# A two-layer hybrid attention block: attention products with the values as the stationary operand, probabilities scaled before them, and branch parts summed in PSUM

## The reference, cut to what matters

```python
y_a = _dsa_attention(...) @ w_branch_a[l]    # 4 heads, one key and value; 64 keys chosen by an index score
y_b = _moba_attention(...) @ w_branch_b[l]   # 4 heads, each with its own keys and values
# branch C: 8 heads in 2 groups; three softmaxes each, weighted by gates
o = g[..., 0:1] * o_c + g[..., 1:2] * o_s + g[..., 2:3] * o_w
```

## Time and profile before

| what | value |
|---|---|
| median of 3 runs | 1232.95 us (1232.95 to 1233.24) |
| the profiled execution | 1232.73 us, of which the span is 1230.8 us |
| PE busy | 1205.6 us (98%) |
| DVE busy | 720.9 us (59%) |
| ACT busy | 577.0 us (47%) |
| DMA, mean over the span | 172 GB/s |
| granted clock of TensorE | 0.999 of full speed |

### The profile page before, as it was taken

The page is one execution under the profiler, slowest core; times in us unless marked ns, Lnnn a source line. Parts: engine busy times, 40 slices in busy tenths (PEclk is TensorE's granted clock), DMA queues, the critical chain, the costliest instruction groups (busy, mean ns, idle before and its releaser), DMA issues.

```text
span 1230.8 us, 18004 instructions
## 1 busy us (share of the span) xinstructions
PE 1205.6 (98%) x6079; PEld 1004.4 (82%) x6079; DVE 720.9 (59%) x800; ACT 577.0 (47%) x733; POOL 47.5 (4%) x83
## 2 busy tenths in 40 slices
PE   5999999999999999999999999999999999999997
PEld 4888888888888888888878888888888888888886
DVE  3545456757775764545455545476676675645454
ACT  5444445446554354343454443454556535443433
POOL 2000000001000100000000000000000020000000
PEclk9999999999999999999999999999999999999999
DMA  6655554764333546555546555646543235655552
GB/s 221 236 176 198 174 200 138 226 214 138 103 104 136 171 157 213 177 190 185 173 139 233 176 194 181 204 152 191 193 145 104 104 137 171 205 182 193 180 195 86
DMA packets 148011, 212.17 MB, mean 172 GB/s; under 512 B 7936, under 2 KB 109424, under 8 KB 147952
## 3 DMA queue, kind: packets, MB, share of 16 engines
q1 hardware_dynamic: 146192, 209.97, 51.3%
q10 hardware_dynamic: 1760, 1.43, 0.4%
HBM read 210.33 MB, written 1.05 MB: 172 GB/s over the span
## 4 chain that ended last, share of the span: by engine, by line
PE 96%; DVE 1%; issue 1%; DMA 1%; ACT 0%; ACTq 0%; POOL 0%; DVEq 0%; SPq 0%; POOLq 0%
PE ps L1049 28%; PE ps L1051 28%; PE ps L1050 28%; PE ps L1276 3%; PE ps L1121 2%; PE ps L1229 1%; PE ps L1253 1%; PE ps L1065 1%; DMA raw<-in_ffn_w_up_dram 1%; PE ps L1292 1%; PE ps L1170 1%; DVE gates L641 0%; PE ps L1222 0%; PE ps L1174 0%; PE ps L1187 0%
## 5 line engine op out<-in xcount | busy, mean ns | idle before, releaser
L391 DVE TENSOR_TENSOR wlo<-raw,whi 128x2048 fp32r<-128x2048 f32 (+2 forms) x199 | 445.6, 2245 | 225.1 <-ACT whi L858 213.1
L1049 PE MATMUL ps<-whi,ht_hi 128*128 128x512 f32 (+1 forms) x1248 | 492.1, 394 | 4.5 <-DVE ht_lo L400 4.5
L1051 PE MATMUL ps<-whi,ht_lo 128*128 128x512 f32 (+1 forms) x1248 | 484.2, 388 | 0.0
L1050 PE MATMUL ps<-wlo,ht_hi 128*128 128x512 f32 (+1 forms) x1248 | 483.3, 387 | 0.0
L858 ACT ACTIVATE whi<-raw 128x2048 fp32r<-128x2048 f32 (+2 forms) x199 | 372.8, 1879 | 175.0 <-PE ps L1051 168.3
L1049 PEld LDWEIGHTS ps<-whi,ht_hi 128*128 128x128 f32 x1248 | 235.1, 188 | 50.4 <-DVE ht_lo L400 5.1
L1051 PEld LDWEIGHTS ps<-whi,ht_lo 128*128 128x128 f32 x1248 | 234.9, 188 | 49.1
L1050 PEld LDWEIGHTS ps<-wlo,ht_hi 128*128 128x128 f32 x1248 | 235.4, 189 | 45.3
L1049 PE MATMUL ps<-whi,at_hi 128*128 128x512 f32 x320 | 124.9, 390 | 0.0
L1051 PE MATMUL ps<-whi,at_lo 128*128 128x512 f32 x320 | 124.7, 390 | 0.0
L1050 PE MATMUL ps<-wlo,at_hi 128*128 128x512 f32 x320 | 124.5, 389 | 0.0
(11 more groups left out here) (150 smaller groups left out, 642.5 us busy)
## 6 DMA issues: line engine op xcount, KB each, us to landing
raw<-in_ffn_w_gate_dram SPq DMA_DIRECT2D x89, 512.0 KB, 3.7
raw<-in_ffn_w_up_dram SPq DMA_DIRECT2D x89, 512.0 KB, 4.7
raw<-in_ffn_w_down_dram SPq DMA_DIRECT2D x88, 512.0 KB, 3.8
raw<-in_w_in_dram SPq DMA_DIRECT2D x88, 512.0 KB, 4.4
raw<-in_w_out_dram SPq DMA_DIRECT2D x16, 512.0 KB, 3.9
raw<-in_w_branch_c_dram SPq DMA_DIRECT2D x8, 512.0 KB, 4.0
w_k<-in_cmp_w_k_dram SPq DMA_DIRECT2D x4, 512.0 KB, 6.6
raw<-in_w_branch_b_dram SPq DMA_DIRECT2D x4, 512.0 KB, 5.2
```

Of the source, the lines that this page charges most:

```text
L391: nc.vector.tensor_tensor(wlo[:, n, 0:w], raw[:, n, 0:w], whi[:, n, 0:w].bitcast(F32), ALU.subtract).then_inc(lo_done, 1)
L1049: nc.tensor.matmul(o, xh, wh, start=start, stop=False)
L1050: nc.tensor.matmul(o, xh, wl, start=False, stop=False)
L1051: return nc.tensor.matmul(o, xl, wh, start=False, stop=stop)
```

## The change

1. `weighted` is turned round. For each half of the keys and each of two heads, 64 columns of values are loaded as weights, and the turned probabilities stream past, 512 columns (first half of the keys) or 256 (second half). Head 0 of a couple writes partitions 0 to 63, head 1 partitions 64 to 127. Part B, whose heads have separate values, takes twice as many products of half the width. The result has the head's columns on partitions, as the branch matrices want it.
2. The division by the sum, and C's gates, move ahead of the product: `scaled` on DVE replaces `normed` and multiplies the probabilities, head by head, in eight instructions for each part (four of 128 elements, four of 256).
3. C, S and W of a group of heads are summed in PSUM. The order becomes I, C, B, S0, W0, S1, W1, A. C's product goes to the S parts, two of 256 columns in each.
4. `turn_out` for the attention outputs (16 transposes) is gone. `heads_out` (ACT) and `heads_rest` (DVE) split each finished bank, two of them in positions 4 and 6, two after position 9.
5. Order: the exponentials of the first half start after the first of the two maxima, the copies of pieces 0, 1 and 2 and the turning of pieces 1 and 2 move in each position, maxima come ahead of the copy on DVE.
6. The second quarter of the compressor's key matrix now lies in the space of the rotated inputs. SP loads it after all of them are turned, ahead of slab 18.

```diff
-PAIRS = ["I", "C", "B", "S0", "S1", "W0", "W1", "A"]
+PAIRS = ["I", "C", "B", "S0", "W0", "S1", "W1", "A"]
+ENDS = ["B", "W0", "W1", "A"]
...
-            def normed(l, e):
+            def scaled(l, e, t):
                 pair, b = PAIRS[e], e % 2
-                dve.wait_ge(o_ps, l * 7 + e)
                 own(l)
                 if pair == "C":
+                    dve.wait_ge(exp_done, l * 2 + 2)
...
+                    step(nc.vector.tensor_tensor(src, src, rden[:, b, :].unsqueeze(2).broadcast_to([P, 16, CPAD]),
+                                                 ALU.mult), ("scaled", e, 0))
                     return
+                dve.wait_ge(exp_half, l * 12 + 2 * (e - 2) + t + 1)
+                rd = rden[:, b, 4 * t:4 * t + 4]
+                step(nc.vector.reciprocal(rd, den[:, b, 4 * t:4 * t + 4]))
+                if pair not in "AB":
+                    g, br = int(pair[1]), 1 if pair[0] == "S" else 2
+                    own(l)
+                    step(nc.vector.tensor_tensor(rd, rd, cgt3[:, t, 4 * g:4 * g + 4, br], ALU.mult))
                 own(l)
+                for h in range(4):
+                    pv = prob_view(b, t)[:, h, :]
+                    step(nc.vector.tensor_scalar(pv, pv, rden[:, b, 4 * t + h:4 * t + h + 1], None, ALU.mult),
+                         ("scaled", e, t))
+            def heads_rest(l, n):
+                dve.wait_ge(heads_hi, l * 4 + n + 1)
+                hi, lo = (v[:, :, :].rearrange("p j c -> p (j c)") for v in heads_parts(n))
+                step(nc.vector.tensor_tensor(lo, ps[:, heads_bank(n), :], hi.bitcast(F32), ALU.subtract), ("heads", n))
...
                 for e in range(NPOS):
-                    if 1 <= e - 2:
-                        normed(l, e - 2)
...
+                    if e == 1:
+                        index_scores(l)
+                    if 0 < e < len(PAIRS):
+                        scaled(l, e, 0)
                     if e > 0:
                         convert(l, S + 17 + e)
+                    if 1 < e < len(PAIRS):
+                        scaled(l, e, 1)
                     for _ in range(rounds[e]):
...
             def weighted(l, e):
+                if pair[0] == "S":
+                    for j in range(2):
+                        hc = 4 * int(pair[1]) + 2 * j
+                        nc.tensor.matmul(o[:, j], v_blk[:, hc:hc + 2, :].rearrange("p h c -> p (h c)"), pc_t,
+                                         start=j == 0, stop=False, skip_group_check=True)
+                opens, vcol = pair in "AB", heads_of(pair)[3]
+                for kt in range(NT):
+                    pt = p_t[:, 2:3, :] if kt else p_t[:, 0:2, :]
+                    pt = pt.rearrange("p f (j e c) -> p e j f c", j=2, e=2)
+                    for js in ([slice(0, 1), slice(1, 2)] if pair == "B" else [slice(0, 2)]):
+                        for h in range(2):
+                            v0 = vcol(2 * js.start + h)
+                            ins = nc.tensor.matmul(o[h * HD:(h + 1) * HD, js, kt:NT, :], pr[:, kt, v0:v0 + HD],
+                                                   pt[:, h, js], start=opens and kt == 0 and js.start == 0,
+                                                   stop=kt == 1 and pair in ENDS, skip_group_check=True)
...
+                    if q == 5:
+                        sp.wait_ge(fill_ps, (l + 1) * NFILL)
+                        sp.dma_start(w1[0][1], rows_cols(cmp_w1_k, l, 8 * P, 8, 0, P)).then_inc(w1_in[0], 16)
                     load_halves(l, S + 13 + q, w_in, 512 * (q % 2), 4, M_G + 512 * (q // 2), 512)
```

More of the change, by code:

```diff
@@ L699, in mixer @@
                 assert done == 16
-                for n in range(4):
-                    turned_rest(l, n)
+                heads_rest(l, 2)
+                heads_rest(l, 3)
                 convert(l, S + 27)
@@ L708, in mixer @@
                 branch_out(l, 0, 2, range(0, 3))
-                turned_rest(l, 4)
-                turned_rest(l, 5)
+                turned_rest(l, 0)
+                turned_rest(l, 1)
                 branch_out(l, 0, 2, range(3, 4))
                 convert(l, S + 30)
-                for n in range(6, 8):
+                for n in range(2, 4):
                     turned_rest(l, n)
@@ L1001, in mixer @@
                         prob_out(l, e - 1, 0)
+                    if e == 4:
+                        heads_out(l, 0)
+                    if e == 6:
+                        heads_out(l, 1)
                     if e > 0:
                         convert(l, S + 17 + e)
[L1004 to L1005 removed]
                     if 0 < e < len(PAIRS):
                         exps(l, e)
[L1008 to L1009 removed]
+                    if e == len(PAIRS):
+                        prob_out(l, e - 1, 2)
                 gates(l, 5)
[L1011 to L1012 removed]
+                heads_out(l, 2)
+                heads_out(l, 3)
                 for m in range(27, 30):
                     convert(l, S + m)
[L1015 removed]
+                for n in range(2):
                     turned(l, n)
                 convert(l, S + 30)
[L1018 removed]
+                for n in range(2, 4):
                     turned(l, n)
@@ L1259, in weighted @@
                 pair = PAIRS[e]
+                n = next(n for n, p in enumerate(ENDS) if PAIRS.index(p) >= e)
                 pe.wait_ge(pt_a, l * PT_ACT + acts_before(e + 1))
-                if e > 1:
-                    wait_step(pe, l, ("pt", e))
-                    wait_step(pe, l, ("norm", e - 1))
-                if pair == "C":
-                    for t in range(NT):
-                        ins = nc.tensor.matmul(ps[:, 7 - t, :], p_t[:, 0, t * P:(t + 1) * P],
-                                               v_blk[:, :, :].rearrange("p h c -> p (h c)"), start=True, stop=True)
-                    ins.then_inc(o_ps, 1)
-                    return
@@ new lines, in weighted, with turn_z @@
+                ins.then_inc(o_ps, 1)
+            def turn_z(l, *pieces):
+                for n in pieces:
+                    wait_step(pe, l, ("z", 1 if n < 2 else 3))
+                    for j in range(2):
+                        for t in range(NT):
+                            k = 2 * n + j
+                            ins = nc.tensor.transpose(ps[:, 4 + n, j * SEQ + t * P:j * SEQ + (t + 1) * P],
+                                                      gate[:, t, 0, k * P:(k + 1) * P], ident[:, :])
+                    ins.then_inc(ot_ps, 1)
```

181 lines of the change are left out of this document (72 added, 109 removed).

## The result

The changed kernel takes 1239.06 us (median of 6 runs, 1238.4 to 1240.23) against 1232.95 (6 runs beside it, 1231.99 to 1236.02). The ratio is 1.0048, with a 95% interval of 1.0035 to 1.0061: it is slower, by 6.1 us, which is clear of the 0.2% that the prediction counted as no change. The forecast was 1232.1 with a range of 1227 to 1237.5, and "slower" had 0.20. The profiled execution took 1239.42 us, its span is 1237.7 us, and the granted clock of TensorE is 0.990 of full speed, where it was 0.999. All six runs show 0.990 or 0.991.

A forecast was written before the change was run, and what follows sets the result against it. PE, busy 98%, was taken as the bound. Its 7.9 us saving a layer goes nearly all into two waits for DVE, leaving 0.8 us in all: 1232.73 to 1231.9, plus 0.2 for the median, 1232.1 us; range 1227 to 1237.5.

The forecast's parts named there:

- PE's saving: Attention products 1.6 us a part instead of 2.63, and 16 output transposes gone: PE does 7.9 us less a layer.
- VectorE's prices and sum: DVE's multiplications at 0.21 and 0.27 us; its work from B's scaling to the mask sums to 53.6 us.
- The wait: At position 7 PE stands idle for DVE's mask, 6.8 us in each layer.
- C's turning: Early in the layer, PE waits 0.7 us for DVE's scaling of C before turning its probabilities.
- the quarter matrix: Its load was expected hidden ahead of `compress`; rival that it is late: 1.0 us a layer, 1234.1 us, chance 0.15.
- The step that failed: From the end of the mask wait to the first branch slab: 24.6 us instead of 27.99.
- the gain of 0.4 us a layer: The branch slab starts at 384.6 instead of 384.99, nearly all of PE's saving going into two waits; 0.8 us in all.
- a rule on VectorE's prices: Skill's errata figure for DVE multiplications, 0.13 and 0.19 us, each part 0.6 us cheaper; set aside for a trace row.
- The rivals: Cheap scaling (0.22), one element per cycle (0.09), heads not overlapping (0.06), late quarter matrix (0.15).
- VectorE at one element per cycle: DVE's scaling ahead of the mask runs at single rate, losing 3.6 us a layer: 1240.1 us, chance 0.09.
- L627's row: Trace row of a one-tensor DVE instruction, 384 elements in 0.359 us, taken as twice the rate: 0.067 us for 128.
- A mean of 59%: DVE's busy share of the whole span in the profile before; in position 6 it was busy 9.80 of 11.5 us.

The follow-up runs named there:

- Experiment 1: Changed kernel with 9 selection rounds in place of 16 (those of positions 5 and 6 left out), so the mask comes early: 1218.03 us.
- experiment 10: Changed kernel with GpSimd's gate multiplications of positions 3 and 5 held until the mask is made: 1235.9 us.
- experiment 2: Changed kernel with 30 unused products filling PE's wait ahead of A's mask: 1233.46 us.
- experiment 4: Changed kernel with 4 unused products ahead of each layer's first transposes and 8 behind them: 1236.29 us.
- Experiment 6: Changed kernel with 22 unused products in the mask wait and position 6's slab remainder moved behind the selection rounds on DVE: 1231.43 us.
- experiment 3: Changed kernel with position 7's slab ahead of A's scores, and the slabs of positions 8 and 9 ahead of the products they followed: 1224.76 us.
- experiment 5: Changed kernel with the slabs of positions 7 to 9 moved earlier on PE and position 6's slab remainder behind DVE's selection rounds: 1218.42 us.
- experiment 7: Changed kernel with only the first of four heads scaled in the five parts ahead of the mask: 1226.12 us.
- experiments 8: Changed kernel with slabs moved earlier, position 6's remainder late, and eight unused products behind each layer's first transposes: 1216.65 us.
- experiment 9: Control: the kernel before the change, with eight unused products behind each layer's first transposes: 1230.43 us.

## Why the prediction was wrong, by its own steps

**PE's saving: right.** A part's products take 1.45 us (forecast 1.6, before 2.63), and the transposes are gone. Experiment 1 shows it in the time: 1218.03 us when the mask is early.

**VectorE's prices and sum: right in mechanism, a little short, and helped by luck.** 0.20 and 0.27 us against 0.21 and 0.27. From B's scaling to the mask it was 54.4 us instead of 53.6. The positions came to 7.6, 10.0, 11.7, 11.8 and 13.3 us against 7.8, 9.65, 11.5, 11.2 and 13.5. The term that was missing is GpSimd's gate work, 0.5 us in position 3 and in position 5 (experiment 10). The mask was ready at 360.08, forecast 359.9. That the two agree to 0.2 us is luck in part: the changed kernel's profile starts 0.6 us earlier (19.50 against 20.08 us), and measured from the start of its own mixer the mask is 0.7 us later than forecast in layer one and 0.8 in layer two.

**The wait: right.** 7.2 us in each layer, forecast 6.8. C's turning waited 0.5 (forecast 0.7), and `compress` for nothing, so the quarter matrix was in time.

**The step that failed** is the one behind the wait: "Behind that wait, to the first branch slab, it was 384.99 - 357.00 = 27.99 us. It is now + 0.44 - 2 x 1.03 - 1.76, 24.6 us." I priced the wait by its length and took the work behind it at the speed that rows before show, though no row of the mixer before has such work behind seven idle microseconds. With the wait filled it is just 24.6 us (experiment 2). With PE idle the windows from 357 to 363 us show the lower level, and it is 26.2 in layer one and 26.8 in layer two. That is 1.6 and 2.1 us. With the mask's 0.7 and 0.8 it turned the gain of 0.4 us a layer into a loss of 1.9 in the first and 2.5 in the second.

The trace before did hold one place of the kind, unread: the program's start, where PE waits 6.7 and 3.1 us with eight transposes between, and the first slab's products then start 0.43 us apart instead of 0.23. It is a start-up, with hardly any work of PE before it, and a window over 15 to 20 us gives a clock of 1.00 there. So the pitch of the products was the only sign.

```profile
9.83 1.97 PE L1065 MATMUL ps<-ident,x 128*128 128x128 f32 x8 [6.71 <-POOLq L784]
...
14.89 0.79 PE L1049 MATMUL ps<-whi,ht_hi 128*128 128x512 f32 x1 [3.09 <-DVE ht_lo L400]
15.48 0.63 PE L1050 MATMUL ps<-wlo,ht_hi 128*128 128x512 f32 x1
```

The Trainium skill (TensorE: Matmul & The Clock Gate, HAM oscillation) says that a PE that waits falls back to half rate and begins its next stretch of work slow. The windows above agree for this wait of 7 us: 0.50 from 357 to 363 us. I had weighed a rule on VectorE's prices, and passed over this one, by which the forecast wait itself had a second price.

**The gap between the layers** was in no step. The stretch through it cost 3.1 us, again at the lower level (622 to 630 us). Where the clock holds there the loss is gone (experiment 2), or most of it, less the filler's own delay (experiment 4). The two mixers (1.6 and 2.1 us) and the gap (3.0) explain what lies between the changed kernel and experiment 2: 6.7, less 0.5 by which the changed kernel's profile started earlier, against 6.2 between the two profiles' spans and 5.6 between the medians. What is left of the miss, 1233.46 against 1232.1, is within the 1.5 us by which the two masks came late, and GpSimd's share of 1.0 us a layer covers that.

**The rivals.** None of them was the cause. The slower side had one mechanism of the right place and sign, VectorE at one element per cycle. It did not happen: the multiplication's two lengths differ by 0.07 us for 128 elements, as L627's row had said. The measured 1239.06 lies near that rival's 1240.1 by coincidence.

**What stays open** is why the clock falls in the gap in some executions of a kernel and not in others. All six runs of the changed kernel have 0.990 or 0.991. Experiment 6 lost it nine times in ten, and experiment 3 probably three times in four (told from the clocks of whole executions). How long PE waits there doesn't decide it: in the profiles the two waits of the gap add up to 2.6 to 2.7 us where the clock held (the kernel before, experiments 1, 2 and 3) and to 2.7 to 2.9 where it fell (the changed kernel, experiments 5, 6, 7 and 10), with 2.73 us (experiment 3) among the first and 2.67 (experiment 10) among the second. The same goes for the waits of 2.7 us in experiment 7. The cost differs too: against the kernel before, the stretch through the gap took 1.6 us (experiment 7) to 3.1 us more (the changed kernel). Experiment 2 never lost it, and the kernel before seldom: two of its runs, 1236.07 and 1235.99 us, have 0.995. The eight products close the question in practice (experiments 8 and 9), but they don't answer it. Whether a slab moved into the gap would do as well was not tried.

## What to carry to other kernels

Before work is moved to the second engine, add up that engine's queue up to its next hard handover. A mean of 59% said nothing here, the sum of 53.6 us all. Here a wait of the engine that bounds the kernel cost its length and the half clock behind it: 1.6 to 2.9 us for waits of about 7 (the changed kernel, experiments 4 and 10), and 0 or 1.6 for a wait of 2.7 (experiment 7). The wait isn't shown to bring on the second loss, in the gap between the layers: that one came in experiment 5 too, where nothing waits for the mask. Then look for work of that engine which doesn't depend on the handover and put it ahead (experiments 3, 5 and 8): the same change that lost 6 us wins 16.7 against the kernel before beside it with the slabs in another order and the gap covered. The eight products alone give the kernel before 2.5 of this (experiment 9), so 13.8 belong to the change and its order.

## What the runs showed of the hardware

- After TensorE's 7 us without work its clock is at 0.50, and more microseconds, in which it works, are at that level too: some three in layer one of the changed kernel, some six in layer one of experiment 4. After an idle stretch of 1.8 us (experiment 3) the clock held in both layers, 0.23 us for 512 columns in bf16. After 2.7 us (experiment 7) it held in layer one, and in layer two it fell to 0.50 once the mask's products were through.
- GpSimd's one-tensor multiplications slow VectorE's short ones: 1.14 to 1.47 us for four of 256 elements and 0.17 to 0.36 for a gate of four elements. The Trainium skill (GPSIMD Engine Reference, 1. Specifications) says that the two engines share their way into SBUF. Experiment 10 agrees for these two rows.
- Four products with 64 weight columns, two at a time side by side on the halves of the partitions, take 1.45 us for 1536 columns of float32, entry and exit included. One after the other they would need 2.6 by the earlier trace rows.
- The program's first slab runs at half speed in the kernel before: a product every 0.43 us from 14.89 to 19.75, against 0.23 with the eight bf16 products of experiment 9 in front, though the window from 0 to 20 us gives a clock of 1.00 in both. The pitch of the products tells more there than that column.
